# A hybrid decoder step on one core: sample states of the linear attention restructured, cache copies issued in other places

## Chip, core and metric

The kernel runs on one core of one Trainium2 chip. The metric is the time of one launch in device microseconds; lower is better. The core has a matrix engine (PE, with a separate weight-load row PEld in the profile), a vector engine (DVE), a scalar engine (ACT), a general engine (POOL) and a sequencer for transfers (SP). Sixteen DMA engines serve three queues here: q1 is fed by SP, q10 by ACT and q0 by POOL. PE's clock has two levels, 1.2 and 2.4 GHz; the profile gives the granted share of 2.4 GHz (0.50 is 1.2 GHz).

## The reference, cut to what matters

One decoder layer is computed for a prompt of 512 tokens and for 8 samples of one token each, with shared weights. Three parts bear on the change.

```
# _layer: gated linear attention (GLA), for each of the 8 samples and 4 heads
S = S * jnp.exp(blast)[..., None] + einsum('bjhd,bjhv->bhdv', kd, vc)   # state 128 x 256, one token
o = einsum('bihd,bhdv->bihv', qc * exp(b), S)      # for one token: q times the new state
o_gla = _rmsnorm(o, gla_norm_g) * silu(gr)         # norm over the 256 values of a head
# _dilated_sample: the window caches move up by one position
new_buf = jnp.stack([kall, vall], axis=2)[:, kall.shape[1] - Lb:]
```

For a sample with one token the state of a head is decayed by a factor per row, the outer product of a key (128 long) and a value (256 long) is added, the new state is an output, and a query reads it. The caches of the three window groups (128, 512 and 1024 positions, 4 KB each) come out shifted by one position for all 8 samples: 8 copies of 508 KB, 8 of 2044 KB, and 16 of 2046 KB, 54 MB, straight from input to output in device memory.

## The kernel before

All large products go through one stream of weight units. A unit `u` of `U` is up to 1 MB in one of two slots of `wraw`, loaded by SP (`issue`, `load`, L299). ACT makes a high part (`split_hi`, L313), DVE the rest (`split_lo`, L326), and PE multiplies in three passes (`three_pass`, L342, 128x260 tiles of 520 tokens, two halves; 24 matmuls are half a tile, 48 a tile of 128 output columns). SP asks for unit u once unit u-2 of the same slot has been split (or, for an `ada` unit, read by PE at L477). ACT evacuates a tile in `copy_tiles` (L391), and in that function the split of the next unit stands before the tiles of this one, so a late weight load holds up everything behind it on ACT.

Between the pieces of the stream a side stage is woven by `Between`: each engine has a generator for the stage, and one step of it runs at each place, which is half a tile in this part. The stages run in the order GLA_IN (8 units, each followed by an `ada` unit), GLA (11 units), att0, att1, att2 (9, 6 and 4 units), gates and output, up projection (22 units in a loop), down projection (16 halves of 11 blocks, 66 matmuls of `gH`/`gL` each, one weight load of 704 KB each). Blocks end in a barrier of all engines.

The sample states are the last steps of GLA: steps 31 to 40 of `GLA_STEPS`, counted from 0, in the last three units. In step b PE reads the state of sample b-1 with `read_out` (L865: for each head two matmuls with the state as weights, 128x128, and one column of queries), then makes the outer products of sample b (L875: one row of `kmask`, a copy of the 8 keys with all but one row zeroed by DVE at L992, against `vtS`, 8x256). DVE decays and adds in `Sring` (L997), POOL loads states and stores new ones through two slots (L1043, L1034), each load waiting for the store of two samples before and for PE's read. After the last sample DVE squares, PE sums with `ones` (L884), ACT takes Ln and Exp, DVE scales.

The cache copies are a list `moves`; `move_cache` issues the next one from ACT's queue. `stream_act` calls it at the start of every unit of GLA, att0, att1 and att2 (30 calls), and the down projection calls it twice per output tile until the list is empty (3 left). The list begins with the convolution state (88 KB), then the small window, the middle one, the large one.

## Time and profile before

| | us |
|---|---|
| median of 3 runs | 1409.94 (1408.94 to 1410.36) |
| profiled execution | 1409.59 |
| its span, first to last instruction | 1407.9 |
| PE busy | 1291.5 (92%) |
| DVE busy | 613.4 (44%) |
| ACT busy | 471.9 (34%) |
| POOL busy | 102.0 (7%) |
| granted PE clock, mean | 0.94 |
| stretch of the sample states (start of the first outer products to the end of the last read) | 348.5 to 418.9 |

Times within the span are counted from its start. The 1.7 us between span and execution lie outside of all instructions. A busy PE is not PE at full speed: at the low clock the same matmul lasts longer and counts as busy all the same, so the rows of the granted clock belong beside those of busy time.

### The profile page before, as it was taken

The page shows a single profiled execution, that of the slowest core. Times are in us where ns is not written, and L with a number is a line of the kernel's source. Part 1 is how long each engine was busy: PE and PEld are TensorE (multiplying, and loading weights), DVE is VectorE, ACT ScalarE, POOL GpSimd, SP SyncE. Part 2 cuts the span into 40 slices and gives each one's busy share as a digit, 9 for nine tenths or more (in the row PEclk, how much of TensorE's full clock was granted, in tenths as well). Part 3 has the DMA queues.
Part 4 walks back from the last instruction along what each step waited for, and adds up shares of the span by engine and source line. Part 5 has one row for each costly group of instructions (what it writes and reads, how often), then busy time and mean ns, then how long its engine had stood idle before and what let it go on. Part 6 is the DMA issues. An engine that isn't in the chain of part 4 may idle for free. (4 is left out here: it accounts for less than half of the span.)

```text
span 1407.9 us, 23505 instructions
## 1 busy us (share of the span) xinstructions
PE 1291.5 (92%) x9887; PEld 1192.6 (85%) x9887; DVE 613.4 (44%) x966; ACT 471.9 (34%) x737; POOL 102.0 (7%) x184
## 2 busy tenths in 40 slices
PE   5699999999998999999988678999699999999997
PEld 3479998898997899799787458999599999999996
DVE  0633134454322244334433836555756565652332
ACT  1572243344012444144243115332633333321212
POOL 1000000000111000010121101100000000010000
PEclk9689999999778999999999778999799999999998
DMA  7535442324657764773674747853233333346221
GB/s 227 195 120 180 150 137 94 108 80 154 232 187 275 238 223 164 247 254 132 220 258 144 263 143 243 287 180 104 61 93 93 91 94 93 93 132 195 83 82 61
DMA packets 164194, 225.63 MB, mean 160 GB/s; under 512 B 7164, under 2 KB 147830, under 8 KB 162684
## 3 DMA queue, kind: packets, MB, share of 16 engines
q1 hardware_dynamic: 148532, 123.76, 28.4%
q10 hardware_dynamic: 1424, 54.52, 10.5%
q0 software_dynamic: 14160, 46.22, 9.6%
q8 instruction: 60, 0.98, 0.3%
q14 instruction: 18, 0.15, 0.0%
HBM read 198.76 MB, written 80.23 MB: 198 GB/s over the span
## 5 line engine op out<-in xcount | busy, mean ns | idle before, releaser
L342 PE MATMUL ps<-actH,whi 128*128 128x260 f32 x2064 | 449.8, 300 | 24.9 <-DVE actL L554 17.8
L342 PE MATMUL ps<-actH,wlo 128*128 128x260 f32 x2064 | 427.0, 289 | 0.0
L342 PE MATMUL ps<-actL,whi 128*128 128x260 f32 x2064 | 426.7, 289 | 0.0
L342 PEld LDWEIGHTS ps<-actH,whi 128*128 128x128 f32 x2064 | 330.1, 196 | 67.5 <-issue 54.8
L342 PEld LDWEIGHTS ps<-actL,whi 128*128 128x128 f32 x2064 | 330.6, 196 | 0.0
L342 PEld LDWEIGHTS ps<-actH,wlo 128*128 128x128 f32 x2064 | 329.8, 195 | 0.0
L326 DVE TENSOR_TENSOR wlo<-wraw,whi 128x512 fp32r<-128x512 f32 (+3 forms) x95 | 141.0, 1497 | 180.3 <-ACT whi L313 179.9
L313 ACT ACTIVATE whi<-wraw 128x512 fp32r<-128x512 f32 (+3 forms) x95 | 119.5, 1275 | 135.8 <-PE ps L342 81.3
L391 ACT ACTIVATE arena<-ps 128x520 f32<-128x520 f32 x76 | 45.4, 600 | 267.5 <-PE ps L342 267.5
L342 PE MATMUL ps<-gH,whi 128*128 128x260 f32 x352 | 71.2, 283 | 1.2 <-DVE wlo L326 1.1
L342 PE MATMUL ps<-gH,wlo 128*128 128x260 f32 x352 | 70.8, 282 | 0.0
L342 PE MATMUL ps<-gL,whi 128*128 128x260 f32 x352 | 70.6, 282 | 0.0
L2034 DVE TENSOR_TENSOR wlo<-wraw,whi 128x2048 fp32r<-128x2048 f32 x22 | 50.4, 2292 | 18.0 <-ACT whi L1979 18.0
L1383 ACT ACTIVATE arena<-arena 128x128 f32<-128x128 f32 (+1 forms) x96 | 39.9, 417 | 53.7 <-DVE arena L1360 53.7
L342 PEld LDWEIGHTS ps<-gH,whi 128*128 128x128 f32 x352 | 54.1, 188 | 1.6 <-DVE wlo L326 1.3
L342 PEld LDWEIGHTS ps<-gL,whi 128*128 128x128 f32 x352 | 54.3, 188 | 0.0
L342 PEld LDWEIGHTS ps<-gH,wlo 128*128 128x128 f32 x352 | 54.1, 188 | 0.0
L496 DVE COPY arena<-ps 128x256 f32<-128x256 f32 x24 | 10.1, 422 | 77.6 <-PE ps L477 77.5
L1979 ACT ACTIVATE whi<-wraw 128x2048 fp32r<-128x2048 f32 x22 | 41.8, 1902 | 0.0
L1354 DVE SCALAR_TENSOR_TENSOR arena<-ps,arena 128x512 f32<-128x512 f32 (+1 forms) x32 | 20.9, 653 | 39.4 <-PE ps L1305 39.4
L477 PE MATMUL ps<-wraw,scP 128*32 128x256 f32 x384 | 30.9, 447 | 5.4 <-DMA wraw<-in_w_ada 5.4
L1986 ACT ACTIVATE arena<-arena 128x520 f32<-128x520 f32 x22 | 14.1, 641 | 63.7 <-DVE arena L2051 63.7
(308 smaller groups left out, 1504.1 us busy)
## 6 DMA issues: line engine op xcount, KB each, us to landing
wraw<-in_w_in SPq DMA_DIRECT2D x38, 1024.0 KB, 5.4
out_win_s<-in_cache_win ACTq DMA_DIRECT2D x16, 2046.0 KB
wraw<-in_w_ada SPq DMA_DIRECT2D x24, 1024.0 KB, 5.5
wraw<-in_w_up SPq DMA_DIRECT2D x44, 512.0 KB, 4.6
out_win_s<-in_cache_win ACTq DMA_DIRECT2D x8, 2044.0 KB
raw_gates<-arena SPq DMA_DIRECT2D x24, 260.0 KB, 5.0
arena<-raw_gates POOLq DMA_DIRECT2D x24, 260.0 KB, 4.6
wraw<-in_w_down SPq DMA_DIRECT2D x16, 384.0 KB, 3.6
```

The source lines that it names most:

```text
L313: ins = act.activation(whi[:, v % 2, c], wraw[:, u % 2, c], ACT.Copy)
L326: ins = dve.tensor_tensor(wlo[:, v % 2, c], wraw[:, u % 2, c], whi[:, v % 2, c].bitcast(F32), ALU.subtract)
L342: last = pe.matmul(ps[:, 2 * (n % 2) + a, 0:HT], wt, X[:, k0 + j, a * HT:a * HT + HT], start=begin and j == 0 and wt is hi and X is H, sto ...
L391: act.activation(halves(to), banks(n), ACT.Copy).then_inc(tile_read["act"], 1)
L477: last = pe.matmul(ps[QC * j:QC * j + QC, 7, 0:2 * P], scP[:, k, :], wraw[:, u % 2, 2 * k * P:2 * (k + 1) * P], start=half == 0, stop=half ...
L496: dve.tensor_copy(rows[:, a % 2, :], ps[:, 7, 0:2 * P]).then_inc(ada_tok, 1)
L1354: dve.scalar_tensor_tensor(sv, ps[:, 4 + n % 2, 0:nh * J].rearrange("p (h k) -> p h k", k=J), SCALE, biasT[:, hs, lo:hi], ALU.mult, ALU.ad ...
L1383: last = act.activation(sv, sv, ACT.Exp, bias=bnd[:, c % 2, b0 + AE:b0 + AE + 1], accum_out=bnd[:, c % 2, b0 + AE + 1:b0 + AE + 2])
L1979: act.activation(whi[:, vn % 2, :], wraw[:, (up0 + 1 + d) % 2, :], ACT.Copy).then_inc(hi_ready, 1)
L1986: act.activation(sg5, acc, ACT.Sigmoid).then_inc(s("ffn_sig"), 1)
L2034: dve.tensor_tensor(wlo[:, vn % 2, :], wraw[:, (up0 + 1 + d) % 2, :], whi[:, vn % 2, :].bitcast(F32), ALU.subtract).then_inc(lo_ready, 1)
```

## The change

The list of copies is reordered and issued elsewhere. Eight of 2 MB (large window) go out at the starts of the eight GLA_IN units, six of 2 MB (middle window) in the first six GLA units, five small ones in att0, three in att1, none in att2; two of the middle and eight of the large window and the convolution state follow in the down projection, one before each of its first eleven splits.

In the sample states the outer products leave PE. The 8 value rows are written to device memory once (`vd`), and POOL loads each sample's row back onto all 128 partitions (`vwide`), beside its state. ACT multiplies `vwide` by the key, which is a scale per partition, DVE decays and adds as before, from SBUF only. `Sring` has four slots instead of two; four samples are requested at once at the start, and later ones when the store of the slot has landed. PE reads a state with one matmul per head: the state is now the moving side (256 columns), and the weights are 32 columns of `qS`, zero but for the sample's own, so that row b of four groups of 32 partitions accumulates over the samples. The norm then works on rows: ACT squares with a sum, the chain Ln, Exp and Newton follows, DVE scales, and PE transposes twice.

Several semaphores are merged under new names with offsets (`late_in`, `slot_in0` to `slot_in3`, `stored0`, `stored1`); the counts waited for are the same events.

```
-        moves = [(o["conv_s"][:, 0, :], w["state_conv"][:, 1, :])]
+        window = [[] for _ in range(NG)]
...
+        M_GLA, M_ATT = 6, (5, 3)
+        moves = window[2][0:8] + window[1][0:M_GLA] + window[0] + window[1][M_GLA:] + window[2][8:]
+        moves.append((o["conv_s"][:, 0, :], w["state_conv"][:, 1, :]))
...
-            for u in us:
-                move_cache(act)
+            for j, u in enumerate(us):
+                if j < n_moves:
+                    move_cache(act)
...
+        SD = 4
+        Sring = at(10400, SD, GH * GDV)
+        vwide = at(18656, SD, GH * GDV)
+        qS = at(22752, GH, NS * QC)
...
             def read_out(b):
                 pe.wait_ge(s("gs_new"), b + 1)
                 for h in range(GH):
-                    for vt in range(2):
-                        col = (2 * h + vt) * NS + b
-                        last = pe.matmul(ps[:, 6, col:col + 1], Sring[:, b % 2, GDV * h + P * vt:GDV * h + P * vt + P],
-                                         qS[:, h, b:b + 1], start=True, stop=True)
+                    last = pe.matmul(ps[QC * h:QC * h + QC, 6, 0:GDV], qS[:, h, QC * b:QC * b + QC],
+                                     Sring[:, b % SD, GDV * h:GDV * h + GDV], start=b == 0, stop=b == NS - 1,
+                                     tile_position=(0, QC * h))
...
-                pe.wait_ge(s("kmask"), b + 1)
-                for h in range(GH):
-                    last = pe.matmul(ps[:, 4 + h // 2, GDV * (h % 2):GDV * (h % 2) + GDV],
-                                     kmask[:, b % 2, GDK * h:GDK * h + GDK], vtS[:, GDV * h:GDV * h + GDV],
-                                     start=True, stop=True)
-                last.then_inc(s("kv_outer"), 1)
                 yield
...
+            for b in range(NS):
+                slot_landed(act, "gs", b % SD, 32 * (b // SD + 1))
+                for h in range(GH):
+                    v = vwide[:, b % SD, GDV * h:GDV * h + GDV]
+                    last = act.activation(v, v, ACT.Copy, scale=gk[:, h, TP + b:TP + b + 1])
+                last.then_inc(s("kv_outer"), 1)
+                yield
+            act.wait_ge(s("gs_read"), NS)
+            act.activation(oS, ps[:, 6, 0:GDV], ACT.Square, accum_out=ssS).then_inc(s("o_sq"), 1)
...
+                pool.wait_ge(s("kvs"), 1)
+                pool.dma_start(vd, vtS).then_inc(s("v_spilled"), 16)
...
+                for b in range(SD):
+                    load_state(b)
+                for b in range(NS):
                     pool.wait_ge(s("gs_new"), b + 1)
                     pool.dma_start(o["gla_s"][b].rearrange("h p v -> p h v"),
+                                   Sring[:, b % SD, :].rearrange("p (h v) -> p h v", h=GH)).then_inc(s(f"stored{b % SD}"), 16)
+                    if 1 <= b <= NS - SD:
+                        pool.wait_ge(s(f"stored{(b - 1) % SD}"), 16 * ((b - 1) // SD + 1))
+                        pool.wait_ge(s("gs_read"), b)
+                        load_state(b + SD - 1)
...
                 for u in GLA_IN:
+                    move_cache(act)
                     copy_tiles(act, u, DESTS[U[u]["kind"]], U[u]["m0"], between)
                 between.finish()
-                stream_act(act, GLA, AQKV[0], gla_act(act), GLA_STEPS)
+                stream_act(act, GLA, AQKV[0], gla_act(act), GLA_STEPS, M_GLA)
```

PE in the sample states, before: 24 matmuls of the stream, then the read of one sample (L865) and the outer products of the next (L875). Two rows of the stream stand here on each side.

```order
L342 MATMUL ps<-actL,whi 128x260 x2
L342 MATMUL ps<-actH,wlo 128x260 x2
L865 MATMUL ps<-arena 128x1 x8
L875 MATMUL ps<-arena 128x256 x4
L342 MATMUL ps<-actH,whi 128x260 x2
```

The same place in the changed kernel:

```order
L364 MATMUL ps<-actL,whi 128x260 x2
L364 MATMUL ps<-actH,wlo 128x260 x2
L887 MATMUL ps<-arena 32x256 x4
L364 MATMUL ps<-actH,whi 128x260 x2
```

Eight small matmuls and four outer products have become four matmuls on 32 output partitions each.

POOL at the start of the sample states, before: two states are requested, and from then on stores (L1034) and loads alternate.

```order
L1029 DMA out_gla_p<-arena 128x256 x4
L1043 DMA arena<-in_state_gla 128x4x256 x2
L1034 DMA out_gla_s<-arena 128x4x256
L1043 DMA arena<-in_state_gla 128x4x256
L1034 DMA out_gla_s<-arena 128x4x256
L1043 DMA arena<-in_state_gla 128x4x256
```

The same place in the changed kernel; `sample_values` is `vd`, and L1053 is the load of a value row onto all partitions.

```order
L1046 DMA out_gla_p<-arena 128x256 x4
L1051 DMA arena<-in_state_gla 128x4x256
L1053 DMA arena<-sample_values 128x1024
L1051 DMA arena<-in_state_gla 128x4x256
L1053 DMA arena<-sample_values 128x1024
L1051 DMA arena<-in_state_gla 128x4x256
L1053 DMA arena<-sample_values 128x1024
L1051 DMA arena<-in_state_gla 128x4x256
L1053 DMA arena<-sample_values 128x1024
L1061 DMA out_gla_s<-arena 128x4x256 x2
L1051 DMA arena<-in_state_gla 128x4x256
L1053 DMA arena<-sample_values 128x1024
```

Eight transfers of 512 KB now stand in a row before the first store, and each later sample has two.

ACT at the start of the down projection, before: three copies, then splits (L313) and squares (L522) alone.

```order
L268 DMA out_win_s<-in_cache_win 32x16368
L313 ACTIVATE whi<-wraw 128x1408
L268 DMA out_win_s<-in_cache_win 32x16368
L313 ACTIVATE whi<-wraw 128x1408
L268 DMA out_win_s<-in_cache_win 32x16368
L313 ACTIVATE whi<-wraw 128x1408 x2
L522 ACTIVATE arena<-arena 128x520
L313 ACTIVATE whi<-wraw 128x1408 x2
```

In the changed kernel, from its third copy on:

```order
L290 DMA out_win_s<-in_cache_win 32x16368
L335 ACTIVATE whi<-wraw 128x1408
L290 DMA out_win_s<-in_cache_win 32x16368
L335 ACTIVATE whi<-wraw 128x1408
L545 ACTIVATE arena<-arena 128x520
L290 DMA out_win_s<-in_cache_win 32x16368
L335 ACTIVATE whi<-wraw 128x1408
L290 DMA out_win_s<-in_cache_win 32x16368
L335 ACTIVATE whi<-wraw 128x1408
```

A copy now stands before every split up to the tenth.

## Rows read from the trace of the kernel before

**Rows 1.** The page, part 2: granted clock in 40 slices of 35.2 us.
```profile
PEclk9689999999778999999999778999799999999998
```

**Rows 2.** One stretch: busy time (x instructions) per engine, clock, DMA, GB/s.
```profile
375.00:400.00 25.00, 25.00 (x129) 23.05 (x129) 6.18 (x15) 1.25 (x3) 4.12 (x6) 0.65 0.42 143
```

**Rows 3.** Timeline of PE, sample states: start, length, engine, line, operands, count.
```profile
389.41 1.84 PE L865 MATMUL ps<-arena 128*128 128x1 f32 x16
391.18 2.61 PE L875 MATMUL ps<-arena 8*128 8x256 f32 x8
...
399.09 1.92 PE L865 MATMUL ps<-arena 128*128 128x1 f32 x16
...
418.88 0.48 PE L342 MATMUL ps<-actH,whi 128*128 128x260 f32 x2
...
421.81 0.53 PE L884 MATMUL ps<-arena,cst 128*128 128x32 f32 x4
```

**Rows 4.** Groups by line, 90 to 200 us: count, busy, mean ns.
```profile
L477 PE MATMUL ps<-wraw,scP 128*32 128x256 f32 x128 | 8.6, 385 | 0.0
```

**Rows 5.** Timeline of ACT, sample states.
```profile
347.58 1.28 ACT L919 ACT_TABLE_LOAD   x1
348.88 0.23 ACT L919 ACTIVATE arena<-arena 128x32 f32<-128x32 f32 x1
349.01 0.59 ACT L391 ACTIVATE arena<-ps 128x520 f32<-128x520 f32 x1
```

**Rows 6.** Timeline of DVE, sample states.
```profile
351.03 1.64 DVE L997 SCALAR_TENSOR_TENSOR arena<-arena,ps 128x256 f32<-128x256 f32 x4
```

**Rows 7.** The page, part 3: queue, packets, MB, share of 16 engines over the span.
```profile
q1 hardware_dynamic: 148532, 123.76, 28.4%
q10 hardware_dynamic: 1424, 54.52, 10.5%
q0 software_dynamic: 14160, 46.22, 9.6%
```

**Rows 8.** The page, part 6: count, KB each, median us from issue to landing.
```profile
arena<-in_state_gla POOLq DMA_DIRECT2D x8, 512.0 KB, 4.3
```

**Rows 9.** Timeline of POOL, start of the sample states.
```profile
345.03 1.53 POOL L1043 DMA_DIRECT2D arena<-in_state_gla  x2 [19.19 <-DVE arena L976]
```

**Rows 10.** Timeline of ACT, down projection.
```profile
1269.09 0.52 ACTq L268 DMA_DIRECT2D out_win_s<-in_cache_win  x1
1282.80 1.38 ACT L313 ACTIVATE whi<-wraw 128x1408 fp32r<-128x1408 f32 x1 [12.34 <-DMA wraw<-in_w_down]
```

**Rows 11.** The chain that ended last, down projection: start, us, what.
```profile
1263.36 19.41 DMA wraw<-in_w_down
...
1285.97 103.32 PE ps L342 x858
```

**Rows 12.** Timeline of PE, GLA_IN and first steps of GLA.
```profile
121.54 1.07 PE L477 MATMUL ps<-wraw,scP 128*32 128x256 f32 x16
...
134.68 1.07 PE L477 MATMUL ps<-wraw,scP 128*32 128x256 f32 x16
...
200.90 1.16 PE L812 MATMUL ps<-cst,arena 128*128 128x128 f32 x8 [0.40 <-ACT arena L892]
```

**Rows 13.** Timeline of ACT, start and end of GLA_IN; in brackets idle time before.
```profile
83.11 1.91 ACT L313 ACTIVATE whi<-wraw 128x2048 fp32r<-128x2048 f32 x1 [6.87 <-DMA wraw<-in_w_in]
...
190.47 1.30 ACTq L268 DMA_DIRECT2D out_conv_s<-in_state_conv  x1
...
196.93 1.92 ACT L313 ACTIVATE whi<-wraw 128x2048 fp32r<-128x2048 f32 x1 [5.81 <-DMA wraw<-in_w_in]
```

**Rows 14.** Timeline of SP, end of GLA_IN.
```profile
191.49 21.67 SPq L299 DMA_DIRECT2D wraw<-in_w_in  x4
```

**Rows 15.** Timeline of PE, start of att0.
```profile
436.53 1.21 PE L1157 MATMUL ps<-arena 33*8 33x384 f32 x2 [3.26 <-DVE arena L1180]
```

**Rows 16.** Waits of DVE, 760 to 800 us: total us, times, longest.
```profile
DVE arena L1429 <- DMA arena<-in_cache_win: 7.0, 2, 6.8
```

More of the change, by code:

```diff
@@ L235, in s, with slot_in, slot_landed @@
             return S[name]
+        E0 = 16 * 3
+        E1 = E0 + 16 * 2
+        E2 = E1 + 16 * 2
+        E3 = E2 + 16 * 4
+        SLOT0 = {"gs": (0, 0), "vc": (0, 64), "cmb": (3, 64), "raw": (0, 96)}
+        CONV0 = 32
+        def slot_in(ring, i):
+            return s(f"slot_in{SLOT0[ring][0] + i}")
+        def slot_landed(eng, ring, i, n):
+            first, before = SLOT0[ring]
+            eng.wait_ge(slot_in(ring, i), (before if first + i < 4 else 0) + n)
         class Chain:
@@ L430, in stream_pe, with stream_act @@
             between.finish()
[L432 removed]
+        def stream_act(act, us, dst, work, steps, n_moves, fine=False):
             between = Between(work, steps, us, fine)
[L434 to L435 removed]
+            for j, u in enumerate(us):
+                if j < n_moves:
+                    move_cache(act)
                 copy_tiles(act, u, dst, U[u]["m0"], between)
@@ L709, in program @@
         sq2 = at(21216, 2, 512)
-        ktS, vtS = at(26848, 512, parts=NS), at(27360, D, parts=NS)
+        vtS = at(27360, D, parts=NS)
         ebS = at(28384, 4, NS)
@@ L715, in program @@
         za, zb = Bt, X1
-        Sring = at(18656, 2, 4 * GDV)
-        kmask = at(10400, 2, 512, parts=NS)
-        qS, gS, oS = at(20704, 4, NS), at(20736, 4 * NS), at(20768, 8, NS)
-        sqS, rsS, rsT, rsV, rsR = at(20832, 8, NS), at(20896, 4 * NS), at(20928, 4 * NS), at(20960, 4 * NS), at(20992, 4 * NS)
+        SD = 4
+        Sring = at(10400, SD, GH * GDV)
+        vwide = at(18656, SD, GH * GDV)
+        qS = at(22752, GH, NS * QC)
+        gS, rsS = at(23776, 4 * NS), at(23808, 4 * NS)
+        ssS, rsT, rsV, rsR, rs2 = (at(23840 + 8 * i, 1) for i in range(5))
+        oS, oN = at(24288, GDV), at(24544, GDV)
         QSC = GDK ** -0.5
@@ L798, in gla_pe @@
             pe.wait_ge(ada_read, 16)
-            for m in range(4):
-                last = pe.transpose(ps[0:NS, 4, P * m:P * m + P], gk[:, m, TP:T], ident)
             for m in range(KD):
@@ L881, in gla_pe @@
             yield
-            pe.wait_ge(s("o_sq"), 5)
+            pe.wait_ge(s("o_normed"), 1)
             for vt in range(2):
-                last = pe.matmul(ps[:, 7, 0:32], ones, sqS[:, vt:KD:2, :], start=vt == 0, stop=vt == 1)
+                last = pe.transpose(ps[:, 7, P * vt:P * vt + P], oN[:, P * vt:P * vt + P], ident)
             last.then_inc(s("o_summed"), 1)
@@ L920, in gla_act @@
             yield
-            for _ in range(NS + 1):
+            for b in range(NS):
[4 more added lines that the diff above has]
+                last.then_inc(s("kv_outer"), 1)
                 yield
+            act.wait_ge(s("gs_read"), NS)
+            act.activation(oS, ps[:, 6, 0:GDV], ACT.Square, accum_out=ssS).then_inc(s("o_sq"), 1)
             act.wait_ge(s("o_v"), 5)
@@ L1237, in heads_tok_act @@
                 act.wait_ge(s("o_spilled"), 16)
-                for d in range(2):
-                    act.wait_ge(s(f"gs_out{d}"), 16 * (NS // 2))
+                for d in range(SD):
+                    act.wait_ge(s(f"stored{d}"), 16 * (NS // SD))
                 for _ in range(FLIP_GAP):
```

115 lines of the change are left out of this document (50 added, 65 removed).

## The prediction, made before the changed kernel had run

> **What bounds the kernel now.** I read the 40 slices first [rows 1]. The clock stands at 9 nearly everywhere; it is low at the start, in the slices from 352 to 422 us (7, 7) and in the later attention. From 352 to 422 us the sample states run. PE is busy without a gap there, but at 0.65 of its clock, with 129 matmul records in 25 us [rows 2]; so the place is bound by PE, and by what PE does, not by a wait. The timeline shows what that is: beside each half tile of the stream, 1.84 us for reading one sample and 2.61 us for the outer products, and the half tile of 24 stream matmuls between the end of the outer products at 393.79 and the next read at 399.09 lasts 5.3 us [rows 3]. At the end of the place the same half tile takes 421.81 - 418.88 = 2.93 us [rows 3]. Everything else in the kernel is the stream of 128x260 matmuls, which I treat as fixed work; the change can only move what is around it. All sums below are in the profiled execution's frame (span 1407.9, execution 1409.59, which is 0.35 under the median of 1409.94; I take both as equal).
>
> **Part 1, the sample states.** Before: from 348.5 to 418.9 us, 70.4 us for eight half tiles of stream, eight reads, eight outer products.
>
> PE alone after: eight half tiles at 2.93 us and eight reads. A read is four matmuls of 256 columns on 32 output partitions in four column groups. The nearest row is the ada product, eight such matmuls: 128 records, 16 for a unit, are 8.6 us, so 1.08 us a unit and 0.54 us for four [rows 4]. That gives 8 x 3.47 = 27.8 us. The outer products and the low clock, if it is due to them and the single-column reads, are gone.
>
> But PE now has to wait, for three things. The chain of a sample is load, ACT, DVE, PE. ACT: four activations of 128x256; between 0.23 us (128x32) and 0.59 (128x520) [rows 5] I take 0.37, so 1.5 us. DVE: 1.64 us as before [rows 6]; half the operands come from another memory, which I count as nothing. The transfers are the longest. The rates in flight from the queues' rows [rows 7]: q0 moved 46.22 MB in 9.6% of 1408 us, 342 GB/s; q10 54.52 MB in 10.5%, 369 GB/s; q1 123.76 MB in 28.4%, 310 GB/s. A state of 0.524 MB is then 1.53 us of all engines, and a value row onto 128 partitions is taken as the same (no such load stands in the trace: not less than its bytes at the fastest rate here, 1.42 us, and at the other end twice the price, 3.1 us, because 128 reads hit one row of memory; I take 1.53, since a state load has the same bytes and the same 128 destinations). Before the last sample can be computed, 16 loads and 5 stores must pass: 21 x 1.53 = 32.1 us. In the same stretch two weight units of 1.05 MB (3.4 us each at 310 GB/s) and three spills of gates (0.8 us each) share the engines: 9.2 us. With the latency of the first load, 4.3 [rows 8] - 1.53 = 2.8 us, the last pair lands 44.1 us after the request at 345.03 [rows 9], at 389.1. Then 1.5 + 1.64 + 0.54: the last read ends at 392.8 instead of 418.9. **Gain 26 us.** If the engines' share is no bound (other rows above it overlap), PE's own pace does it: first read at 354.8 (the first pair lands at about 351: 345.03, two issues of 0.77 [rows 9], 4.3), then seven times 3.47 and some 2.5 us where ACT's and DVE's splits of a weight unit stand before a sample: end at 382, gain 37. If value rows cost double, 8 x 1.53 = 12 us more: gain 14.
>
> The skill prices a transfer from POOL's queue at about 2 us fixed plus its bytes at 436 GB/s (the Trainium skill, "DMA: Bandwidth & Descriptors", "Anatomy of one DMA"); with that slope the 21 transfers would take 25 us and not 32, and part 1 would gain 33; the trace's landing of 4.3 us [rows 8] is longer than the 3.2 us that the rule gives for one, so I stay with the rows.
>
> After the last read, the norm: Square, a table load 1.28, Ln 0.23, table load 1.28, Exp 0.23 [rows 5], three small DVE steps and a scaling, about 5.1 us by these, and PE stands at its transposes one half tile (2.93 us) later. Before, the step there (L884) only needed DVE and did not wait [rows 3]. **Cost 2 us.** Four transposes of keys at the start of GLA go: gain 0.5. The spill of the values (32 KB on POOL) stands before the stores of prompt states and holds nobody. The memset of `qS` on DVE lies beside ACT's gate chain: 0. Part 1 sums to -24.5 us (-36 to -12).
>
> **Part 2, copies into GLA_IN.** A copy of 2.09 MB takes 5.7 us of all engines at 369 GB/s. It is carried in packets of 38 KB on average, a weight unit in packets of 0.8 KB [rows 7]; the down projection shows what that does: with three copies requested (1258.9, 1259.5 and 1269.09; the last row stands), a load of 704 KB asked for at 1263.36 took 19.41 us [rows 10, 11]. So I let a copy stop a weight load for its whole length. A GLA_IN unit takes PE 13.1 us [rows 12] and asks for two units of weights: 2 x 3.4 + 5.7 = 12.5 us. That fits, barely, with no cost in the middle but for a bubble or two (ACT falls behind in the gate chain of the first units, so two copies come back to back): 1.5 us. At both ends it does not fit. First copy: it is requested right before a split that already waits 6.87 us for its weights, until 83.11 [rows 13]; the load moves back about 3 us, ACT's gate chain with it, and PE's steps need that chain each 4 us: 3 us. Ninth copy (first of GLA): requested where the 88 KB copy goes out now, at 190.47 [rows 13], one us before the weights of 191.49 [rows 14], for which ACT waits until 196.93 [rows 13]; behind that split stand the value rows for which PE waits 0.40 us already [rows 12]. The load's data would start near 193.5 and now start at 196.5: 3.2 us. Sum **+8 us** (2 to 20). In the other five GLA units a unit lasts over 20 us and the copy is covered by that; if the cover were gone each would cost up to 5.7.
>
> **Part 3, copies out of att0 to att2.** At the start of att0 PE waits 3.26 us [rows 15] for DVE, which waits for a table that POOL loads right behind a 2 MB copy. A small copy of 0.52 MB (1.4 us) stands there now, 4.3 us less: the wait is gone, and perhaps some of the low clock behind it. -4. In att2 a 2 MB copy stands before the loads of keys and group outputs; DVE waits 7.0 us in all for such loads, once 6.8 [rows 16], and it then leads for some 40 us, with PE waiting for it. Without the copy DVE is about 4 us earlier: -3.5. Elsewhere PE hardly waits for a transfer. Sum **-7.5 us** (-12 to -1).
>
> **Part 4, copies into the down projection.** A unit is 66 matmuls: 103.32 / 858 x 66 = 7.95 us [rows 11]. A copy and the weights (0.72 MB at 310 GB/s, 2.3 us) need 8.0 us of engines. What was seen is slower: from 1258.9 to 1282.8 the engines did three copies and one load, 19.4 us of work in 23.9, a factor 1.2. So 9.6 us a unit, 1.65 over PE's pace, for seven more units: 11.6, less the slack of a unit (7.95 less the two splits, 3.0): 5 us. **+6.5 us** (0 to 13). ACT cannot run ahead, because each copy stands behind the split before it.
>
> **Sum:** -24.5 + 8 - 7.5 + 6.5 = -17.5 us: **1392 us**. With the ends that go together most likely (loop -30 to -17, copies -2 to +14 in all) its own range is 1381 to 1403.
>
> **Rivals.** R1, the loop runs at PE's pace and the copies are mostly hidden: -35, and parts 2 to 4 together +1: 1376. For it: shares over 1 do occur with copies and loads together; against: q0's rate is an average of loads and stores in flight, and the engines would have to move 12 MB in 35 us beside the weights.
>
> R2, the clock stays low in the loop. PE waits for loads between half tiles, and in the rows the clock is also low where PE waits. At 1.2 GHz a half tile is 5.3 us (above) and a read about 0.9: 8 x 6.2 = 50 us, and the first wait: loop gain 18 instead of 26. With the rest as forecast: 1400. Here the skill speaks against the change (the Trainium skill, "TensorE: Matmul & The Clock Gate", "HAM oscillation — how this bites in real kernels"): bursts of matmuls with a transfer wait between them start each burst at the low clock. In this trace the low clock of [rows 2] comes with no wait at all, so another cause is at work there, and that a wait of 1 to 2 us between bursts of 3.5 brings it is not shown.
>
> R3, slower: transfers of one queue do not overlap as the shares say, and each weight load costs its landing time behind a copy. Then a GLA_IN unit needs 5.7 + 5.4 + 5.4 = 16.5 us (the landing is 196.93 - 191.49 = 5.4 [rows 13, 14]) against 13.1 to 14: about +3 for seven units, 21 with the ends; the down projection 5.7 + 4 + bubbles, +13. Together +34 against -32: 1412, and with a loop as in R2, 1420. It decides from 1.8 us of stall for each of the 18 copies there. For it stands the factor 1.2 of part 4; against it, that a load requested while a copy runs has its latency behind it when the copy ends. R4: that nothing of part 1 arrives since the loop is bound elsewhere has no support, PE being busy at 100% there.
>
> **How the numbers follow.** Forecast 0.50 (1392), R1 0.20 (1376), R2 0.17 (1400), R3 0.13, of which half ends over 1413 and half within a few us of no change. A measurement of this kernel can tell about 0.2% (2.8 us) from no change. Slower by more: 0.07. Within: 0.06 (R3's other half). Faster: 0.87. The range leaves out the fastest part of R1 and R3: 1372 to 1406.
>
> **What would show it.** In the changed kernel's profile: no outer products on PE; clock near 1.00 from 350 to 390 us; the last read 40 to 45 us after the first value load; POOL waits for stores and ACT for loads in the loop. ACT's split waits at 83 and 197 us grow by 3 us, with PE waiting in the steps behind. No wait before the bias products (L1157) in att0. In the down projection ACT waits for weights in units 3 to 10 and PE stalls 5 to 8 us in all, none later. I am wrong if the value loads take over 2 us each, if the clock stays near 0.6 in the loop, or if ACT's waits for weights in GLA_IN grow from unit to unit.

## The result and the profile after

The changed kernel took 1403.45 us (median of 20 runs, 1391.97 to 1411.57) against 1409.8 (1402.08 to 1419.05): ratio 0.9942, 95% interval 0.9917 to 0.9968. The forecast was 1392. The direction was right and the time lies in the stated range, but the gain is 6 to 8 us where 18 were forecast. The profiled execution has a span of 1401.8 us against 1407.9, 6.1 less.

To see where the time went I counted the stream's matmuls (128x260) along the timeline of PE in both traces, 7824 in each, and compared the time at which each of them begins; the stream is the same work in the same order. The differences, changed kernel less kernel before, and beside them what the prediction had for the stretch that ends at the place:

```
place (time before, us)                 difference   in the stretch   forecast
first unit of GLA_IN, 85.6                 -3.0          -3.0            0
second unit of GLA_IN, 101.6               +5.1          +8.1           +3
last unit of GLA_IN, 182.8                +14.3          +9.2           +1.5
first unit of GLA, 204.0                  +21.6          +7.3           +3.2
before the samples, 340.5                 +21.5          -0.1            0
behind them and the norm, 428.0            -2.4         -24.0          -24.5
in att0, 471.2                             -2.6          -0.2           -4
in att2, 737.5                             -3.3          -0.7            0
behind att2 and output, 945.6             -14.0         -10.7           -3.5
end of the up projection, 1256.4          -14.0           0.0            0
end of the down projection, 1386.4         -4.5          +9.5           +6.5
end of the span                            -6.1          -1.6            0
```

The first row is no effect of the change that I can name: in the thirteen profiles of this document the first matmul of the stream begins between 56.9 and 63.0 us.

The large miss is part 2: three stretches that were to cost 8 us cost 24.6. The samples came out as forecast. The timeline of PE has a read (L887) between the half tiles, the outer products are gone, and the last read stands at 414.18; POOL asked for the first state at 366.58:

```profile
376.72 0.64 PE L887 MATMUL ps<-arena 128*32 128x256 f32 x8 [2.21 <-DVE arena L1015]
...
414.18 0.64 PE L887 MATMUL ps<-arena 128*32 128x256 f32 x8 [1.25 <-DVE arena L1015]
419.54 0.44 PE L900 MATMUL ps<-cst,arena 128*128 128x128 f32 x2 [1.66 <-DVE arena L1023]
```

```profile
366.58 0.77 POOL L1051 DMA_DIRECT2D arena<-in_state_gla  x1 [19.23 <-DVE arena L999]
```

From the request to the end of the last read are 48.2 us; the prediction's sum (392.8 - 345.03) was 47.8, before it was 73.9. The transfer engines are full there, which stretches of 10 us show (as in [rows 2]; the last three columns are clock, DMA share, GB/s):

```profile
375.00:385.00 10.00, 8.28 (x61) 7.28 (x62) 4.10 (x10) 4.70 (x10) 1.53 (x2) 0.83 1.04 381
395.00:405.00 10.00, 6.81 (x61) 5.78 (x62) 3.35 (x8) 3.10 (x8) 4.09 (x6) 1.00 1.04 390
405.00:415.00 10.00, 6.68 (x48) 5.43 (x47) 5.63 (x9) 5.15 (x10) 1.34 (x2) 0.83 0.95 342
```

The clock was 0.65 in [rows 2] and is 0.83 to 1.00 now, though PE waits 1 to 3 us in most turns: the low clock of before went with the single-column reads and outer products. Where these stay and only the copies move (below, the copies alone), the clock is 0.66 from 375 to 400 us. Which of the two kinds of matmul goes with it, no run tells.

GLA_IN is where the time went. The timeline of ACT at its start and in the middle (L290 is a copy's issue, L335 a split; these answer to [rows 13]), and that of SP (as [rows 14]):

```profile
74.61 0.65 ACTq L290 DMA_DIRECT2D out_win_s<-in_cache_win  x1
87.38 1.91 ACT L335 ACTIVATE whi<-wraw 128x2048 fp32r<-128x2048 f32 x1 [12.18 <-DMA wraw<-in_w_in]
...
168.18 1.92 ACT L335 ACTIVATE whi<-wraw 128x2048 fp32r<-128x2048 f32 x1 [11.50 <-DMA wraw<-in_w_in]
171.40 0.52 ACTq L290 DMA_DIRECT2D out_win_s<-in_cache_win  x1
184.40 1.91 ACT L335 ACTIVATE whi<-wraw 128x2048 fp32r<-128x2048 f32 x1 [12.35 <-DMA wraw<-in_w_in]
...
204.72 0.52 ACTq L290 DMA_DIRECT2D out_win_s<-in_cache_win  x1
217.23 1.91 ACT L335 ACTIVATE whi<-wraw 128x2048 fp32r<-128x2048 f32 x1 [11.86 <-DMA wraw<-in_w_in]
```

```profile
76.21 0.37 SPq L321 DMA_DIRECT2D wraw<-in_w_in  x1
...
172.45 0.37 SPq L321 DMA_DIRECT2D wraw<-in_w_in  x1
172.86 6.51 SPq L321 DMA_DIRECT2D wraw<-in_w_ada  x1
...
205.74 6.79 SPq L321 DMA_DIRECT2D wraw<-in_w_in  x2
```

In these three turns the copy is asked for 1.0 to 1.6 us ahead of the weights, and the weights land 11.2 us (87.38 - 76.21), 11.95 (184.40 - 172.45) and 11.5 us (217.23 - 205.74) after the request, where it was 5.4 before [rows 13, 14]. That is 5.8 to 6.5 more, a whole copy of 5.7, and not the half of it that I had taken. The transfers between request and landing show why. From 172.4 to 178.3 us the engines carry the copy (q10) and nothing of the weights (q1) that were asked for at 172.45; from 178.4 to 184.4 they carry the weights:

```profile
q10 hardware_dynamic: 32, 2.10, 99.1%
```

```profile
q1 hardware_dynamic: 1733, 1.76, 94.6%
q10 hardware_dynamic: 15, 0.00, 0.1%
```

What the split's lateness does to PE stands in PE's timeline behind the split of 184.40:

```profile
186.95 0.84 PE L779 MATMUL ps<-cst,arena 128*128 128x128 f32 x4 [2.03 <-ACT arena L413]
187.72 1.94 PE L500 MATMUL ps<-wraw,scP 128*32 128x256 f32 x16
...
192.78 0.64 PE L364 MATMUL ps<-actH,wlo 128*128 128x260 f32 x2
...
194.31 0.40 PE L364 MATMUL ps<-actH,whi 128*128 128x260 f32 x2
```

ACT stood at the split and let PE wait 2.03 us for its evacuation (L413); behind the wait a pair of stream matmuls takes 0.64 us instead of 0.40, and the `ada` product 1.94 instead of 1.07 [rows 12], until 193.7. The wait of 2 us costs 5.3 in all.

The down projection went as forecast in kind. The chain that ended last, and PE's wait for it (before, one of 1.14 us, at the 1285.97 of [rows 11]):

```profile
1273.28 15.33 DMA wraw<-in_w_down
...
1292.39 15.05 DMA wraw<-in_w_down
...
1311.22 14.69 DMA wraw<-in_w_down
...
1329.02 55.76 PE ps L364 x462
```

```profile
PE ps L364 <- DVE wlo L348: 7.1, 4, 2.7
```

Four waits, 7.1 us in all, come in every second unit. The first and the third, 1.96 and 2.71 us long, are followed by matmuls at the low clock, which makes up the rest of the 9.5.

### The profile page after: what moved, and what is told of

It reads as the page before. It is cut to its first block and busy times, and to the rows that moved or that the text cites. A ratio compares the mean times of both kernels' runs of the same rounds, so it can differ in the third digit from the quotient of the medians.

```text
span 1401.8 us, 23268 instructions
## 1 busy us (share of the span) xinstructions
PE 1254.4 (89%) x9753; PEld 1159.0 (83%) x9753; DVE 611.6 (44%) x958; ACT 483.8 (35%) x770; POOL 107.0 (8%) x193
## 3 DMA queue, kind: packets, MB, share of 16 engines
q0 software_dynamic: 15344, 50.45, 10.7%
## 5 line engine op out<-in xcount | busy, mean ns | idle before, releaser
L335 ACT ACTIVATE whi<-wraw 128x512 fp32r<-128x512 f32 (+3 forms) x95 | 119.5, 1274 | 218.7 <-DMA wraw<-in_w_in 92.3
L413 ACT ACTIVATE arena<-ps 128x520 f32<-128x520 f32 x76 | 45.1, 599 | 162.2 <-PE ps L364 162.2
L1770 DVE SCALAR_TENSOR_TENSOR arena<-ps,mod,arena 128x260 f32<-128x260 f32 x16 | 7.8, 488 | 67.7 <-PE ps L364 67.7
```

What stands on the lines that cost most here:

```text
L335: ins = act.activation(whi[:, v % 2, c], wraw[:, u % 2, c], ACT.Copy)
L413: act.activation(halves(to), banks(n), ACT.Copy).then_inc(tile_read["act"], 1)
L1770: dve.scalar_tensor_tensor(xT[:, q, 0:HT], a, g, xT[:, q, 0:HT], ALU.mult, ALU.add)
```

## The experiments

All kernels are timed against the kernel before on the same chip, five rounds each; "the changed kernel" is that of the change. Positions along the stream are given as in the table above. The groups of runs come from different chips, so kernels of different groups are compared by their ratios. The code is cut to the lines that matter; three points stand for what is left out.

**The samples alone.**

```
-        moves = window[2][0:8] + window[1][0:M_GLA] + window[0] + window[1][M_GLA:] + window[2][8:]
-        moves.append((o["conv_s"][:, 0, :], w["state_conv"][:, 1, :]))
+        moves = [(o["conv_s"][:, 0, :], w["state_conv"][:, 1, :])] + window[0] + window[1] + window[2]
...
-                if j < n_moves:
-                    move_cache(act)
+                move_cache(act)
...
                 for u in GLA_IN:
-                    move_cache(act)
```

> The changed kernel's sample states with the copies of the kernel before (same list, same places, so two or three copies of 2 MB stand beside the samples again, and none in GLA_IN). Theory A, the stages add up: from the first request of a state to the last read 48 us in the changed kernel (366.58 to 414.82) against 73.9 before (345.03 to 418.9), plus 5.7 to 11.4 for one or two copies beside it: 54 to 60 us, GLA_IN as before (last split at about 197), all in all 12 to 20 us under the kernel before, a span of 1388 to 1396, ratio 0.986 to 0.991. Theory B, the restructured states gain only when nothing shares the transfer engines: the loads starve behind the copies as weight loads do, the stretch is 65 us or more, and the span is within 8 us of before.

Measured: 1386.14 us, ratio 0.9837 (0.9804 to 0.987), span 1383.5. The gain is a little over theory A's: 21.1 us in the stretch of samples and norm, and within 2 us of before everywhere else. Of the two copies beside the samples, the second (386.17) comes when the last loads are nearly through; the first (359.30) shows as a wait of 8.85 us before the fifth read:

```profile
366.87 0.64 PE L885 MATMUL ps<-arena 128*32 128x256 f32 x8 [0.21 <-DVE arena L1013]
379.44 1.08 PE L885 MATMUL ps<-arena 128*32 128x256 f32 x8 [8.85 <-DVE arena L1013]
```

Yet the stretch from request to last read is 51 us (54 to 60 were expected) against 48.2: half of the copy's time is hidden. So "no copy beside the samples" was worth about 3 us, and the restructuring alone beats the whole change by 15.

**The copies alone.** The kernel before with the changed list and places (the first, third and fourth group of the change's diff, applied to it).

> The kernel before with the changed kernel's list and places of copies; the sample states as before. Theory A (the copies alone cost what the two traces say by place in the stream: 21 to 25 us in GLA_IN and the start of GLA, -10 to -12 in att0 to att2, +9 in the down projection): span 1407.9 + 20 = 1428, ratio 1.010 to 1.018, and the stretch of the samples still 70 us. Theory B (the copies beside the samples had slowed the old loop too, by bandwidth or by the clock): the stretch falls to 60 us or less and the span is 1418 or less.

Measured: 1424.14 us, ratio 1.0107 (1.0063 to 1.0152), span 1424.6; the samples' stretch is unchanged (+1.6). Theory A holds. By medians, states alone -22.0, copies alone +16.0, sum -6.0; the change measured -6.4. The two halves add up (with intervals of some 5 and 6 us to each side), so the missing gain is the price of the copies' new places. By place that price is smaller than I expected, 18 us in GLA_IN and the start of GLA instead of 21 to 25, and 7.5 in the down projection instead of 9; att0 to att2 give back 7 instead of 10 to 12.

**GLA_IN without copies.**

```
-        moves = window[2][0:8] + window[1][0:M_GLA] + ...
+        moves = window[1][0:M_GLA] + ...
                 for u in GLA_IN:
-                    move_cache(act)
```

> The changed kernel without the eight copies of GLA_IN: they are not made at all, so half of the large window's cache is missing from the output; all other copies stand where they stood. Theory A (these copies and the two at the head of GLA cost what the stages show): the 16.3 us that the stream has lost by the split at 200 come back, of the 8 us at the next split perhaps half; span 1401.8 - 16 to -24 = 1378 to 1386, ratio to before 0.979 to 0.985. Theory B (only the first and the ninth copy cost, as the prediction had it, the rest of the loss is scatter of one profile): span 1392 or more.

Measured: 1390.01 us, ratio 0.9865 (0.9836 to 0.9894), span 1386.8: between the two. The eight copies are left out, so half of the large window is missing from the output. Up to the end of GLA_IN the stream loses nothing (-1.0 against before), and the copy at the head of GLA costs 7.7 us alone, as much as with eight copies ahead of it. It is asked for at 189.47, 1.0 us ahead of the weights (190.49), and the split waits:

```profile
201.91 1.91 ACT L335 ACTIVATE whi<-wraw 128x2048 fp32r<-128x2048 f32 x1 [11.79 <-DMA wraw<-in_w_in]
```

**The eight copies at another point of ACT's program.**

```
                 act.activation(halves(to), banks(n), ACT.Copy).then_inc(tile_read["act"], 1)
+                if move and m == 0:
+                    move_cache(act)
...
                 for u in GLA_IN:
-                    move_cache(act)
-                    copy_tiles(act, u, DESTS[...], U[u]["m0"], between)
+                    copy_tiles(act, u, DESTS[...], U[u]["m0"], between, move=True)
```

> The changed kernel with each of the eight copies of GLA_IN issued after the first tile of the unit has been copied out of PSUM, some 6 us after the split, instead of before the unit: it then stands behind the request for the next weights instead of ahead of it. All else as in the changed kernel. Theory A (the place is what costs: all these units use one slot, so the next load can only be asked for after the split, and a copy asked for just ahead of it delays each turn): the splits of GLA_IN are 13 to 14 us apart, and the span is 10 to 16 us under the changed kernel's, 1386 to 1392, ratio to before 0.984 to 0.989. Theory B (the transfer engines are full: 3.4 + 3.4 + 5.7 = 12.5 us of work and the factor 1.2 of the down projection give 15 us a unit): the splits stay 15 us apart and the span is 1398 to 1402.

Measured: 1389.84 us, ratio 0.9857 (0.9827 to 0.9886), span 1385.3: 12 to 14 us under the changed kernel. From its third unit on the splits are 13.2 to 14.5 us apart, and GLA_IN loses 1.0 us (-6.2 in its first unit, -5.2 in its last), all with the same eight copies. So the engines' capacity is no bound (theory B falls): what costs is the place. But the copies do not stand where I said. The timelines of ACT and SP in this kernel:

```profile
149.50 1.92 ACT L335 ACTIVATE whi<-wraw 128x2048 fp32r<-128x2048 f32 x1 [5.67 <-DMA wraw<-in_w_in]
150.56 0.52 ACTq L290 DMA_DIRECT2D out_win_s<-in_cache_win  x1
162.78 1.92 ACT L335 ACTIVATE whi<-wraw 128x2048 fp32r<-128x2048 f32 x1 [4.95 <-DMA wraw<-in_w_in]
```

```profile
153.76 0.37 SPq L321 DMA_DIRECT2D wraw<-in_w_in  x1
158.20 0.82 SPq L321 DMA_DIRECT2D wraw<-in_w_ada  x1
```

The copy is 3.2 us ahead of the request, not behind it, and the weights land in 9.0 us. In the changed kernel the lead was 1.0 and the landing 11.95 (172.45), or 2.8 and 9.15 (143.36 to 152.51). The further the copy is ahead in these, the less of it falls into the load's time; a landing of 9 fits into the 13.1 to 14 us of PE's unit beside split and low part (about 4.3 us from a split to the next request), one of 11.5 to 12 doesn't. A second difference is the `ada` load: asked for 0.41 us behind the weights in the changed kernel (172.86), 4.4 us behind here. The trace of the kernel before speaks against it as the cause: there an `ada` load asked for 0.42 us behind the weights leaves them a landing of 5.39 us (77.65 and 78.07, landed at 83.04). More lead is no help without end: in the later units of two kernels below the copy is 5.4 to 5.9 us ahead of the weights, the `ada` load follows 1.0 us behind the copy and ahead of them, and they land in 9.3 to 10.1 us.

**The copies of GLA at that point too.**

```
             for j, u in enumerate(us):
-                if j < n_moves:
+                if j < n_moves and not behind:
                     move_cache(act)
-                copy_tiles(act, u, dst, U[u]["m0"], between)
+                copy_tiles(act, u, dst, U[u]["m0"], between, move=behind and j < n_moves)
```

> The changed kernel with the copies of GLA_IN and of GLA all issued behind the first tile's evacuation of the unit. In the traces so far the ninth copy (the first of GLA, asked for just ahead of the weights) costs 7 to 8 us with and without the eight copies before it. Theory A (place): this cost goes, the span is 6 to 8 us under that of the kernel in which only GLA_IN's copies stand behind (1385.3), so 1377 to 1380; ratio to before 0.978 to 0.983. Theory B (the stretch is short of bandwidth, whatever the order, because of the value rows and two weight loads there): it stays within 3 us of 1385.

Measured: 1383.25 us, ratio 0.9815 (0.9779 to 0.9851), span 1382.5. By the ratios this is 6 us less than with GLA_IN's copies alone, though the two intervals overlap, and the span is only 2.8 less where theory A had 6 to 8 (this profile enters GLA_IN 5 us later). What decides is the place itself: the loss at the head of GLA is gone (-0.6 instead of +7.3). Here the copy is truly behind: asked for at 199.06, the weights at 190.43, and the next split (206.71) does not wait. Theory A. The copy is now 1.1 us ahead of another load (200.18), which lands in 11.24 us, as late as those of the changed kernel; but that load is split 21 us after it has landed, and costs nothing. So the place is dear only where the load has no slack.

**Every copy where there is cover.** This is the kernel with both groups moved, with one line changed:

```
-        M_GLA, M_ATT = 6, (5, 3)
+        M_GLA, M_ATT = 8, (9, 6)
```

> As the kernel with both groups of copies behind the evacuation, and the rest spread: 8 large in GLA_IN, 8 middle in GLA, 8 small and one large in att0, 6 large in att1, none in att2, and only one large and the convolution state left for the down projection. Theory A (copies in att1 are covered by 20 us of PE to a unit: six large there cost nothing in the kernel before; eleven in the down projection cost 6 to 9 us): 5 to 8 us under the kernel with both groups behind, span 1370 to 1374, ratio to before 0.973 to 0.978. Theory B (a copy costs some 0.7 us wherever it is): the same time as with both groups behind.

Measured: 1380.29 us, ratio 0.9794 (0.976 to 0.9828), span 1379.0. That is 3 us under the kernel with both groups moved, where theory A had 5 to 8 and theory B nothing; the intervals overlap. The down projection, with two copies left, loses nothing instead of 6.2, and nine copies in att0 lose nothing there (-0.1). In att1 the six large ones lose 1.8 us against before (which had six large ones there too), and seven kernels with three small ones gain 0.8 to 0.9: the cover is not quite whole there.

**Half the rate in the down projection.**

```
-        M_GLA, M_ATT = 6, (5, 3)
+        M_GLA, M_ATT = 6, (5, 6)
...
                     for half in range(2):
-                        move_cache(act)
+                        if half == 0:
+                            move_cache(act)
```

> The changed kernel with three more copies (two middle, one large) in att1, and the eight left for the down projection (seven large, the convolution state) before every second split instead of before each. Theory A (rate: a copy of 2.09 MB and the weights in each 7.95 us of PE ask for more than the engines give, half that rate does not): the down projection, which lost 9.4 us against the kernel before, loses 0 to 2, and the span is 7 to 9 us under the changed kernel's, 1393 to 1395. Theory B (each copy ahead of a weight load costs its delay, as in GLA_IN, whatever the rate; in the down projection two slots alternate): the loss falls only with the number of copies, from 9.4 to about 7.

Measured: 1387.63 us, ratio 0.9859 (0.982 to 0.9898), span 1383.6. Over the down projection the stream gains 1.6 us against before, with seven large copies in it; the splits are 7.9 us apart and wait for PE only:

```profile
1279.49 1.38 ACT L335 ACTIVATE whi<-wraw 128x1408 fp32r<-128x1408 f32 x1 [6.53 <-PE ps L364]
1279.53 0.52 ACTq L290 DMA_DIRECT2D out_win_s<-in_cache_win  x1
1287.42 1.39 ACT L335 ACTIVATE whi<-wraw 128x1408 fp32r<-128x1408 f32 x1 [6.03 <-PE ps L364]
```

Theory A: it is the rate. By the ratios the total is 12 us under the changed kernel, about what the down projection gives (11); but by the spans it is 18, and much of that stands in GLA_IN. Its code there is that of the changed kernel, yet the middle units cost nothing (+0.9 at 101.6, +1.5 at 182.8):

```profile
163.92 0.52 ACTq L290 DMA_DIRECT2D out_win_s<-in_cache_win  x1
165.46 1.92 ACT L335 ACTIVATE whi<-wraw 128x2048 fp32r<-128x2048 f32 x1 [0.89 <-DMA wraw<-in_w_in]
177.96 0.52 ACTq L290 DMA_DIRECT2D out_win_s<-in_cache_win  x1
179.85 1.92 ACT L335 ACTIVATE whi<-wraw 128x2048 fp32r<-128x2048 f32 x1 [1.25 <-DMA wraw<-in_w_in]
```

The request for the weights is at 169.73, so the copy has a lead of 5.8 us, and the landing hardly holds the split. I call this the early course: ACT is paced by PE's tiles, goes through them, issues the copy and then splits. In the changed kernel's profile, the late course, ACT is paced by the weights, has the tiles waiting, and issues the copy after the split, with a lead of 1. I took each course to keep itself up; the repeat below shows that it does not always.

**Fewer value rows.** The rows of samples 4 to 7 are not loaded (and the counts that ACT waits for are lowered to fit), so the states and outputs of these samples are not those of the reference:

```
-                    pool.dma_start(vwide[:, d, :], vd[...]).then_inc(slot_in("gs", d), 16)
+                    if b < SD:
+                        pool.dma_start(vwide[:, d, :], vd[...]).then_inc(slot_in("gs", d), 16)
```

> The changed kernel without the value rows of samples 4 to 7: their loads are left out, ACT multiplies what is left in the slot, so the states and outputs of these four samples are not the reference's. 17 transfers stand between the first request and the last sample's data instead of 21. Theory A (the sum of the prediction: the stretch is bound by the transfer engines at 1.5 us for each 0.5 MB): the stretch from the first state's request to the last read falls from 48.2 to 41 to 43 us, the span by 6. Theory B (bound by the chain of a slot: store, its landing, load, its landing, ACT, DVE, PE): it falls by less than 2 us.

Measured: 1397.16 us, ratio 0.992 (0.9887 to 0.9953), span 1392.1. From the first request (354.77) to the end of the last read (398.59) are 43.8 us, 4.4 less than 48.2, and samples and norm gain 28.4 instead of 24.0. Four transfers less make 1.1 us each: nearer to A (6) than to B (under 2). The transfers bound the stretch, though not alone.

**The changed kernel once more, and with two copies moved.**

> The changed kernel itself once more. Its 20 runs fall into two groups, five from 1392 to 1397 and fifteen from 1402 to 1412, and two kernels with the same GLA_IN lost nothing there between the splits at about 105 and 180 us where the profile of the changed kernel lost 8.9 us. Theory A (two courses of GLA_IN: once ACT is held up by a weight load, the next copy is issued right behind the split and ahead of the next request, which holds ACT up again; if ACT is held by PE's tiles instead, each copy goes out after the weights have landed): the runs again show two groups some 9 us apart, and a profile from the lower one loses under 1.5 us in the middle units. Theory B (all of it is scatter of other stages): no gap between the runs, and the profile's loss in the middle is somewhere between 0 and 9.

```
-                for u in GLA_IN:
-                    move_cache(act)
-                    copy_tiles(act, u, DESTS[...], U[u]["m0"], between)
+                for j, u in enumerate(GLA_IN):
+                    if j >= 2:
+                        move_cache(act)
+                    copy_tiles(act, u, DESTS[...], U[u]["m0"], between, move=j < 2)
```

> The changed kernel with only the first two copies of GLA_IN behind the first tile's evacuation; the other six stand ahead of their units as in the changed kernel. Theory A (the two courses): nothing holds ACT up at the start, so the six others find the course in which they go out after the weights have landed, although their place in the program is the same; GLA_IN loses 0 to 1.5 us to the split at 180, 7 at the ninth copy, and the span is that of the kernel with all eight behind, 1384 to 1389. Theory B (each copy ahead of a request costs its own delay): six eighths of the 8.9 us of the middle remain, and the span is 1391 to 1395.

Measured: the repeat 1401.39 us, ratio 0.9943 (0.9919 to 0.9968), 12 runs from 1391.39 to 1407.29, with 1399.83 between the groups: no clean gap. Its profile loses 4.7, 5.4 and 7.5 us in the three stretches of part 2: it begins in the late course and leaves it after two units. The other kernel took 1394.85 us, ratio 0.9915 (0.9878 to 0.9952), 10 runs from 1389.79 to 1408.85; the first copy costs nothing (0.0), but its profile, one of the slower runs (span 1402.6), is in the late course and loses 7.4 us in the middle. So theory A of both was too strong: there are two courses, but a good start doesn't decide between them, and the times do not fall into two clean groups.

The turn at which it tips can be read in the traces. In four profiles with this GLA_IN (the copies alone, half the rate, fewer value rows, the repeat) the early course begins right behind a turn in which the copy was asked for 1.6 to 2.1 us behind the weights, which then landed in 5.1 to 6.4 us. A copy only 0.2 to 1.2 us behind them does not spare them: landings of 11.2 to 12.9 us in five turns of four profiles. In four of these turns an earlier copy stood 5.5 to 6.1 us ahead as well; the clean case is the fifth, a turn of the kernel with two copies moved (timelines of SP and ACT):

```profile
137.26 0.37 SPq L321 DMA_DIRECT2D wraw<-in_w_in  x1
```

```profile
137.90 0.52 ACTq L290 DMA_DIRECT2D out_win_s<-in_cache_win  x1
148.49 1.92 ACT L335 ACTIVATE whi<-wraw 128x2048 fp32r<-128x2048 f32 x1 [9.99 <-DMA wraw<-in_w_in]
```

What sets in which of the two ways the copy falls at that turn is open; it is a matter of about 1 us.

**The best of these.** The kernel with both groups moved, with these lines changed:

```
-        M_GLA, M_ATT = 6, (5, 3)
+        M_GLA, M_ATT = 8, (9, 3)
...
                     for half in range(2):
-                        move_cache(act)
+                        if half == 0:
+                            move_cache(act)
```

> GLA_IN 8 large and GLA 8 middle copies behind the evacuation, att0 8 small and one large, att1 only three large, att2 none, and four large and the convolution state before every second split of the down projection. Theory A (att2 gains 5 to 8 us where att1's last three units have no copies, 0 to 3 where they have six, as the kernels so far show; thin copies in the down projection cost nothing): the span is 3 to 6 us under the kernel with the copies spread (1379.0), 1373 to 1376, ratio to before 0.974 to 0.978. Theory B (the differences in att2 are scatter of a profile): the same as there within 2 us.

Measured: 1376.94 us (1373.77 to 1382.91), ratio 0.9774 (0.9748 to 0.98), span 1381.2 for its profile, the slowest of its runs. It beats both kernels, and isn't told apart from the one with the copies spread (0.9794). The ratio is the one that theory A gave, but its reason falls: the profile gains 0.2 us in the stretch of att2 and output, with three copies in att1. Across the eleven kernels without copies in att2 the gain there is 0.2 to 10.7 us, mean 5.3, and 1.5 in the one that has them: scatter of att2, and no link to att1 that these profiles show.

## Why the prediction was off, step by step

**Part 1: right.** -24.0 against -24.5; -23.0 to -24.1 in the eight other profiles that have it whole and no copy beside it. The wait for loads, the stores that POOL waits for, and the last read 48.2 us behind the first request were as forecast (the sign "40 to 45 us after the first value load" was not: 47.5 us, and the prediction's own sum gives 47); the norm cost 2.2 (2 forecast). R1 falls by the waits of PE (10.7 us for L887), R2 by the clock of 0.83 to 1.00.

**Part 2: the step that failed.** +8 forecast, bounds 2 to 20; the changed kernel's profile has 24.6, its repeat 17.7, three more profiles with these copies ahead of the units 12.8 to 18.1. The three terms of the sum:
- The first copy, 3 us: 4.7 to 8.1 measured in five profiles. I let the weights' latency run beside the copy and so took half of it; the rows show the landing longer by a whole copy. I had the price of 5.7 us in hand, and had even said that a copy stops a load for its whole length.
- The ninth, 3.2 us: 6.7 to 9.0 in eight profiles, the same slip; the experiment that asks for it behind the weights brings it all back.
- The middle, 1.5 us: 0.1 to 9.2. The sum 3.4 + 3.4 + 5.7 = 12.5 against 13.1 looked at the engines' work per unit. What counts is the loop of one slot: split and low part, 4.3 us in which no weights of this kind can be on their way, then the landing. 4.3 + 9 fits, 4.3 + 11.5 = 15.8 doesn't, and the splits of the changed kernel at 168.18, 184.40 and 200.35 are 16 us apart. The text had the fact (SP asks once the slot is split) and did not use it. R3 had it half: its 16.5 us a unit is near the late course, and its 21 us for the part lies in what was measured; what it added in the down projection did not come.

Why a copy holds a load up so fully: on q10 a packet is 38 KB on average, on q1 0.8 KB [rows 7]. The Trainium skill ("DMA: Bandwidth & Descriptors", "Queues, rings and completion order") says that an engine changes between queues at packets only. The packets agree with it. The copy's 32 packets of 65 KB start in two rounds of 16, some 2.5 to 3 us apart. For the copy of 171.40 above no packet of the weights starts between the two. For that of 137.90, which came while weights were under way, the weights' packets stop at 141.9, 16 of them pass beside the start of the second round, from 144.0 to 144.4, and they go on after 146.5 (transfers from 142 to 146.5 us):

```profile
q10 hardware_dynamic: 16, 1.05, 63.0%
q1 hardware_dynamic: 16, 0.01, 0.9%
```

So in these two the weights got at most one packet for each of the copy's. That the packet size is the reason, no run here shows by changing it.

**Part 3: the sum near, its terms not.** Forecast -7.5, measured -11.6 in this profile, -8.7 in the repeat. The -4 of att0 did not come in any kernel (-1.0 to +0.3 with whole samples): the wait for the table went, as [rows 15] let expect, and a new one stands 20 us later:

```profile
452.55 2.07 PE L1190 MATMUL ps<-arena,cst 128*128 128x512 f32 x2 [5.43 <-DMA arena<-bias_by_distance]
```

PE reaches the place sooner, and the bias tables, which POOL writes out beside the spill of the GLA output and then loads, are late: what was next in the queue I had not asked. The term of att2, -3.5, is -5.3 in the mean of eleven profiles.

**Part 4: right in kind, short in size.** 6.5 forecast; 6.0 to 9.5 in eight profiles with the copies at each split. The waits (7.1 us, 5 to 8 forecast) are right, at units 4, 6, 8 and 10; what is missing is the low clock behind the two longer ones, some 2 to 3 us. At half the rate the cost is nil.

With part 2 at 17 (the mean of the five profiles with these copies ahead of all units, 12.8 to 24.6), att0 at 0, att2 at -5 and the down projection at 7.5 (the mean of eight), the prediction's sum is -24.5 + 17 - 5 + 7.5 = -5: 1405, 1.5 us over the measured time. The terms put in are measured ones, so this says only that nothing large is missing. The error of part 2, 9 us, makes most of the 11 us by which the forecast was off; the att0 and down projection terms add 5, and att2 takes 1.5 of them back.

## What to carry to other kernels

When transfers are to be hidden under a stream of weights, adding up the engines' work per unit is not enough: follow the loop of the buffer (from release to request to landing) and see what the added transfer stands ahead of. Where the load has no slack, a large copy that was asked for 1 us ahead of it, or up to 1.2 us behind it, held it up by a whole copy; with the copy 3 us or more ahead, or 1.6 us or more behind, the loop held, or nearly so. Where the load has slack, the place did not matter. And time the two halves of a change apart: this one was a gain of 22 us and a loss of 16.

## What the runs showed of the hardware

- A copy in 65 KB packets stops a load in 1 KB packets almost entirely: in 5.6 us from the copy's first packet no packet of the waiting load started in one case, and 16 of its 1040 in 4.5 us in the other.
- The same code of GLA_IN cost 0.1 to 9.2 us in its middle units in five profiles (5.4 and 9.2 in the two of the changed kernel itself), as the copies fell 6 us or 1 us ahead of the requests; part of the 20 us between the runs of the changed kernel can come from there.
- A wait of PE of 2.0 us was followed by some 7 us at the low clock and cost 5.3; those of 1.96 and 2.71 us in the down projection began stretches of 0.64 us a pair of 3 to 4 us, while after 1.49 and 0.99 us the pairs stayed at 0.40.
- A value row spread over 128 partitions (512 KB from 4 KB of memory) cost 1.1 us a piece in a full stretch, less than the 1.5 us that the average rate gives for 512 KB.
